# Split products as three matmuls of 256 columns, and new addresses for the weight tiles, in a two-block transformer kernel

## The reference

```
def conv_ffn(h, w_up, conv_w, conv_b, w_down):
    up = causal_dwconv(h @ w_up, conv_w, conv_b)
    a, b = up[..., :FFN_DIM], up[..., FFN_DIM:]
    return (jax.nn.silu(a) * b) @ w_down
```

## Time and profile before

| | |
|---|---|
| time, median of 3 | 2948.65 us (2948.19 to 2951.15) |
| profiled execution, its own time | 2955.68 us |
| its span, first to last instruction | 2953.9 us |
| TensorE busy | 2915.8 us, 99% of the span, 18584 matmuls |
| weight loads busy | 2611.7 us, 88% |
| VectorE / ScalarE / GpSimd busy | 2049.5 / 1311.1 / 69.9 us (69% / 44% / 2%) |
| mean granted TensorE clock | 0.998 of full speed |
| DMA | 531 MB, mean 180 GB/s, about half of the 16 engines' time |

### The profile page before, as it was taken

One profiled execution on the slowest core, in us unless ns is written; L12 is line 12 of the kernel. 1 busy time (PEld: TensorE's weight loads), 2 busy tenths in 40 slices (PEclk: granted clock), 3 DMA queues, 4 the chain that ended last, 5 costly groups with the idle time before them and its releaser, 6 DMA issues.

```text
span 2953.9 us, 47041 instructions
## 1 busy us (share of the span) xinstructions
PE 2915.8 (99%) x18584; PEld 2611.7 (88%) x18584; DVE 2049.5 (69%) x2623; ACT 1311.1 (44%) x1418; POOL 69.9 (2%) x72
## 2 busy tenths in 40 slices
PE   8999999999999999999999999999999999999999
PEld 8898899999988888888888888877988888888888
DVE  6675798877788888885557777637666666665444
ACT  5354423444454444444444345426445444444333
POOL 0000000000001000000000000000000000000000
PEclk9999999999999999999999999999999999999999
DMA  6553334555555555555555555541555555555555
GB/s 233 185 185 134 116 115 157 167 177 190 195 188 196 192 192 196 189 180 186 187 189 202 192 185 177 181 148 72 186 197 187 196 192 191 196 189 180 192 195 185
DMA packets 87998, 531.06 MB, mean 180 GB/s; under 512 B 10080, under 2 KB 10976, under 8 KB 41824
## 3 DMA queue, kind: packets, MB, share of 16 engines
q1 hardware_dynamic: 87904, 529.76, 51.3%
HBM read 527.10 MB, written 2.10 MB: 179 GB/s over the span
## 4 chain that ended last, share of the span: by engine, by line
PE 96%; DVE 3%; ACT 1%; DMA 0%; issue 0%; SPq 0%; DVEq 0%; ACTq 0%
PE bank L594 74%; PE late L594 21%; DVE arena L1703 0%; DVE arena L1700 0%; DVE w_low L1703 0%; DVE half_low L1703 0%; ACT w_high L1219 0%; DVE arena L2005 0%; PE late L1160 0%; DMA ring<-in_w_gates 0%; DMA xT<-in_xT 0%; DVE small L2565 0%; ACT arena L1674 0%; DVE acts_both L1703 0%; DVE arena L2061 0%
## 5 line engine op out<-in xcount | busy, mean ns | idle before, releaser
L1703 DVE TENSOR_TENSOR w_low<-ring,w_high 128x2048 fp32r<-128x2048 f32 (+1 forms) x480 | 1014.2, 2113 | 386.4 <-ACT w_high L1219 382.5
L1219 ACT ACTIVATE w_high<-ring 128x2048 fp32r<-128x2048 f32 (+1 forms) x480 | 849.5, 1771 | 632.9 <-DMA ring<-in_w_down 225.9
L594 PE MATMUL bank<-up_early,w_high 128*128 128x512 f32 x1408 | 487.7, 389 | 0.0
L594 PE MATMUL bank<-up_late,w_high 128*128 128x512 f32 x1408 | 487.3, 389 | 0.0
L594 PE MATMUL late<-acts_both,w_high 128*128 128x512 f32 x1408 | 485.8, 392 | 0.3 <-DVE w_low L1703 0.3
L594 PE MATMUL late<-acts_both,w_low 128*128 128x256 f32 x1408 | 391.7, 278 | 0.0
L594 PE MATMUL bank<-up_late,w_low 128*128 128x256 f32 x1408 | 388.6, 276 | 0.0
L594 PE MATMUL bank<-up_early,w_low 128*128 128x256 f32 x1408 | 388.6, 276 | 0.0
L594 PEld LDWEIGHTS late<-acts_both,w_high 128*128 128x128 f32 x1408 | 264.5, 188 | 58.3 <-DVE w_low L1703 0.6
L594 PEld LDWEIGHTS bank<-up_early,w_high 128*128 128x128 f32 x1408 | 264.3, 188 | 55.1
L594 PEld LDWEIGHTS bank<-up_late,w_high 128*128 128x128 f32 x1408 | 264.3, 188 | 54.8
(11 more groups left out here) (312 smaller groups left out, 4885.0 us busy)
## 6 DMA issues: line engine op xcount, KB each, us to landing
ring<-in_w_up SPq DMA_DIRECT2D x176, 1024.0 KB, 4.7
ring<-in_w_down SPq DMA_DIRECT2D x128, 704.0 KB, 4.0
ring<-in_w_in SPq DMA_DIRECT2D x66, 1024.0 KB, 4.7
ring<-in_w_mix SPq DMA_DIRECT2D x62, 1024.0 KB, 4.8
ring<-in_w_gates SPq DMA_DIRECT2D x96, 512.0 KB, 3.7
ring<-in_w_branch SPq DMA_DIRECT2D x16, 1024.0 KB, 4.8
ring<-in_w_out SPq DMA_DIRECT2D x16, 1024.0 KB, 4.7
ring<-in_w_o SPq DMA_DIRECT2D x16, 1024.0 KB, 4.8
```

The costliest lines, as they stand in the source:

```text
L594: return nc.tensor.matmul(o, lhsT, rhs, start=first, stop=last)
L1219: A(w_high[:, s, 0:cols], ring[:, s, 0:cols], ACT.Copy).then_inc(rounded[s], 1)
L1703: return V.tensor_tensor(o, a, b, op)
```

## The change

Every pair product becomes a triple through `mm3`, including the body of `down`. The bank's second half is no longer written by these products; the copies of it on ScalarE, the adds of the two halves on VectorE and their semaphores (`half_copied`, `gate2_summed`) go, and readers wait for `drained` instead. A pad of 192 bytes behind the ring and a new `arena_pad` move everything behind the ring by 192 bytes: `hT` is at 65856, `arena` at 94784, `w_high` at 192000. Modulo 256 the activations are now at 64, the ring at 128 and `w_high` at 0: lowered weights are 64 off the moving tiles, rounded weights still 192 off, and both halves of the gate units 64 off.

```
+LINE = 16
...
         ring = sb("ring", [P, RING, UNIT])
         ring_base = nc.sbuf_base - RING * UNIT * 4
+        sb("ring_pad", [P, 3 * LINE])
...
-        sb("arena_pad", [P, -nc.sbuf_base % 128 // 4])
+        sb("arena_pad", [P, (hT_base - nc.sbuf_base) % 256 // 4])
...
-            def project_pairs(pairs, waits=None):
-
-                def body(s):
-                    for k in range(KT):
-                        if waits:
-                            waits(k)
-                        c = slice(k * P, (k + 1) * P)
-                        mm(bank[s][:], w_high[:, s, c], pairs[k], k == 0, False)
-                        last = mm(bank[s][:, 0], w_low[:, s, c], pairs[k][:, 0], False, k == KT - 1)
-                    return last
-                return body
...
-                unit_split(project_pairs(pairs, waits))
+                unit_split(project_split(high, low, waits))
...
-                                c = slice(k * P, (k + 1) * P)
-                                mm(bank[4 + b][:], w_high[:, s, c], acts_both[:, :, n], n == 0, False)
-                                last = mm(bank[4 + b][:, 1], w_low[:, s, c], acts_high[:, n], False, n == FF_TILES - 1)
+                                last = mm3(bank[4 + b][:, 0], s, k, acts_high[:, n], acts_low[:, n],
+                                           n == 0, n == FF_TILES - 1)
...
-                unit_split(project_pairs(ups))
-            rounds_split(21, project_pairs(ups))
+                unit_split(project_split(ups_high, ups_low))
+            rounds_split(21, project_split(ups_high, ups_low))
...
-                A(xms[:], bank[s][:, 1], ACT.Copy).then_inc(half_copied, 1)
...
-                link(tt(x, x, bank[4 + b][:, 0:1], ADD))
-                tt(x, x, bank[4 + b][:, 1:2], ADD).then_inc(down_drained[b], 1)
+                tt(x, x, bank[4 + b][:, 0:1], ADD).then_inc(down_drained[b], 1)
...
-                tt(x, bank[s][:, 0], xms[:], ADD).then_inc(drained[s], 1)
+                tt(x, bank[s][:, 0], xrs[:]).then_inc(drained[s], 1)
                 dve.wait_ge(drained[s], units.drained[s].value())
-                link(tt(x, x, xrs[:]))
...
-                tt(o, bank[s][:, 0], in2_rs)
-                tt(xtmp[:], bank[s][:, 1], in2_rs).then_inc(drained[s], 1)
+                tt(o, bank[s][:, 0], in2_rs).then_inc(drained[s], 1)
                 dve.wait_ge(drained[s], units.drained[s].value())
-                return tt(o, o, xtmp[:], ADD)
```

More of the change, by code:

```diff
@@ L270, in build @@
         up_early, up_late = alias("up_early", hT_base, [P, 8, 2, T]), alias("up_late", arena_base, [P, 8, 2, T], 78)
-        ups = [part[:, k] for part in (up_early, up_late) for k in range(8)]
+        ups_high, ups_low = ([part[:, k, n] for part in (up_early, up_late) for k in range(8)] for n in range(2))
         acts_both = alias("acts_both", arena_base, [P, 2, FF_TILES, T], 0)
@@ L661, in _, with merged_out @@
             merges = [0]
-            def merged_out(both):
+            def merged_out(high, low):
                 n = merges[0]
@@ L669, in waits @@
                     pe.wait_ge(merged_lowered, KT * n + k + 1)
-                pairs = [both[:, :, k] for k in range(KT)]
-                unit_split(project_pairs(pairs, waits))
+                unit_split(project_split(high, low, waits))
                 for j in range(3):
-                    unit_split(project_pairs(pairs))
-                rounds_split(3, project_pairs(pairs))
+                    unit_split(project_split(high, low))
+                rounds_split(3, project_split(high, low))
             def project(s):
@@ L1022, in _ @@
             rounds_split(3, branches)
-            merged_out(out_both)
-            raw_unit(lambda waits: project_pairs(ups, waits))
+            merged_out(each(out_high), each(out_low))
+            raw_unit(lambda waits: project_split(ups_high, ups_low, waits))
             for j in range(3):
-                unit_split(project_pairs(ups))
-            rounds_split(21, project_pairs(ups))
+                unit_split(project_split(ups_high, ups_low))
+            rounds_split(21, project_split(ups_high, ups_low))
             down(0)
-            raw_unit(lambda waits: project_pairs(in2, waits), second=True)
-            unit_split(project_pairs(in2))
-            rounds_split(2, project_pairs(in2))
+            raw_unit(lambda waits: project_split(in2_high, in2_low, waits), second=True)
+            unit_split(project_split(in2_high, in2_low))
+            rounds_split(2, project_split(in2_high, in2_low))
             banks_back()
@@ L1500, in round_act, with pair_round @@
                 A(acts_high[:, bass.ds(n, 1)], ACTS[:, bass.ds(n, 1)], ACT.Copy).then_inc(acts_rounded, 1)
[L1502 to L1507, removed]
-                A(xms[:], bank[s][:, 1], ACT.Copy).then_inc(half_copied, 1)
-            def pair_round(i, cols, late, first=False):
+            def pair_round(i, cols, late, convolved, first=False):
                 for j in range(2):
@@ L1515, in pair_round @@
                         root()
-                        act.wait_ge(norm_done, norm[0])
-                    copy_half()
+                    s, _, _, _, _ = units.next()
+                    made = units.drained[s].value()
                     if late[j]:
@@ L1521, in pair_round, with pair_rounds @@
                     round_weights(cols[2 * j + 1])
-                    convs.add()
-                    act.wait_ge(conv_made, convs.value())
+                    if convolved:
+                        convs.add()
+                        act.wait_ge(conv_made, convs.value())
+                    else:
+                        act.wait_ge(drained[s], made)
                     A(cv[:, 2 * j], cv[:, 2 * j], ACT.Silu).then_inc(silu_pair, 1)
-                    copy_half()
+                    units.next()
                     acts.add()
-            def pair_rounds(first, n, late):
+            def pair_rounds(first, n, late, convolved):
                 with act.Fori(0, n) as i:
@@ L1532, in pair_rounds @@
                     acts.enter(i, 2)
-                    convs.enter(i, 2)
-                    pair_round(i + first, [UNIT] * RING, late)
+                    convs.enter(i, 2 * convolved)
+                    pair_round(i + first, [UNIT] * RING, late, convolved)
                 units.leave(n)
@@ L1538, in pair_rounds, with feed_forward @@
                 convs.leave(n)
-            def feed_forward():
+            def feed_forward(convolved):
                 half = SPLIT_UP // 2
[L1542 to L1545, removed]
+                pair_round(0, [UNIT] * RING, (False, True), convolved, first=True)
+                pair_rounds(1, half - 1, (True, True), convolved)
+                pair_round(half, [UNIT] * RING, (True, False), convolved)
+                pair_rounds(half + 1, 20 - half, (False, False), convolved)
                 last = FF_TILES - 2
-                pair_round(21, [UNIT] * 2 + [DOWN * P] * 2, (False, False))
+                pair_round(21, [UNIT] * 2 + [DOWN * P] * 2, (False, False), convolved)
                 act.wait_ge(consumed[(units.pos - 1) % RING], units.consumed[(units.pos - 1) % RING].value())
@@ L1564, in square_of @@
                 norm[0] += 1
+            made2 = []
             for u in range(IN2 + GATES2):
-                units.next()
+                s, _, _, _, free = units.next()
+                made2.append((drained[s], free + 1))
                 if u:
@@ L2210, in low @@
                 def low(n):
-                    lower_raw(n, ups[n][:, 0], ups[n][:, 1], v(gain, n))
+                    lower_raw(n, ups_high[n], ups_low[n], v(gain, n))
                 for n in range(KT):
@@ L2281, in down @@
                     ahead.enter(i, turns=2, drained=0, split=1)
-                    chain.enter(i, 2)
                     turn(i, [DOWN * P] * 8)
@@ L2285, in down @@
                 ahead.leave(7)
-                chain.leave(7)
                 turn(7, [DOWN * P] * 6 + [after] * AHEAD)
@@ L2319, in convolved @@
                 last = stt(o[:, 2:], x[:, 0:T - 2], w(0), o[:, 2:], M, ADD)
-                made_half(last, half)
-            def made_half(last, half):
                 if half == 0:
@@ L2365, in feed_forward @@
                 pairs.leave(20)
-                halves.leave(20)
                 convs.leave(20)
@@ L2600, in _ @@
             residual_raw("g_ffn")
[L2601 removed]
+            feed_forward(scaled, 0, 0)
             down(0)
```

62 lines of the change are left out of this document (24 added, 38 removed).

## The result

The changed kernel takes 3018.36 us (median of 4, 3016.69 to 3026.57) against 2948.42 us before: a ratio of 1.0241, 95% interval 1.0221 to 1.0261. It is slower by 70 us, outside the predicted range (2828 to 2996) and on the side to which I had given 28%.

What follows compares the result with a forecast made beforehand. TensorE was taken as the bound, by matmuls times pace. Terms 0 - 14.1 - 10.2 - 6.8 - 2.7 - 0.4 = -34.2 took the profiled 2955.68 to 2921.5 us (2921 against the median); range 2828 to 2996.

Steps and rivals of the forecast that it cites:

- What bounds the kernel: Whole kernel: TensorE, busy 99% of the span, sets the time by number of matmuls times their start-to-start pace.
- The clean pace of 113.3 ns: Split streams: 256 columns cost 113.3 ns without a clash, so three matmuls take 340 ns.
- faster than a clean pair: Rival, 20%: the new addresses beat a pair's pace, a triple takes 328 ns, total 2834 us.
- Pairs to triples at 340: Pair products, 5664 k tiles: as triples they stay at 340 ns, price 0, bounds 0 to +75.5 us.
- The triples that exist: Existing triples, 1056 k tiles: from 353.3 to 340 ns each, -14.1 us.
- The gates: Gates' half units, 768 k tiles: 360 to 340 ns, 15.4 us of TensorE time, two thirds counted, -10.2 us.
- The slow stretches: First down product and second block's gates: k tiles at 350 return to 340 ns, -6.8 and -2.7 us.
- The last add: Very end of the kernel: the last tile's two adds, 0.88 us, become one, -0.4 us.
- The addresses do nothing: Rival, 11%: paces follow matmul order alone, new triples run at 353.3 ns, old triples and gates unchanged, 3021 us.
- only a linear gain: Rival, 17%: each load's better offset saves only 3.3 ns, a triple takes 350 ns, slower at 2994 us.
- The fixed cost of 2.5 ns a matmul: Rival, 7%, using 2.7 ns: a third matmul adds that, a triple takes 342.7 ns, total 2941 us.

Runs made afterwards that it cites:

- experiment 5: The changed kernel with its two offsets exchanged (rounded weights 64 off, lowered and gates 192 off): 2926.73 us, ratio 0.9916 to the kernel before.
- 13: The kernel of experiment 5 with the gates' rounded half units 64 off as well: 2921.67 us, ratio 0.9899 to the kernel before.
- experiment 10: The changed kernel with a plain float32 matmul of 128 columns ahead of each of the up products' 168 looped units: 2988.58 us, ratio 1.0116 to the kernel before.

## Why the prediction was wrong

- **What bounds the kernel: right.** TensorE is busy for 99% of the span in each of the fifteen profiles and idle for 35 to 40 us of it (38.1 before, 37.2 with the change), at a granted clock of 0.996 to 0.999, the 2.4 GHz level: no wait accounts for the differences, and pace by number of k tiles does.
- **The clean pace of 113.3 ns: right.** 340 is the lowest pace of any form at any offsets, and the triples of experiments 5 and 13 run at it from end to end. The rival "faster than a clean pair" (20%) is refuted as far as these offsets reach.
- **Pairs to triples at 340: wrong, and this is the step that failed**, named as the weak point: "in a stream with locked paces removing the one clash can clear all three". I had seen in the earlier trace rows that a stream has several steady paces, and still gave each form and offset one price. At the changed offsets there are two, 340 and 356.7, and the stream is in the slower one almost everywhere: 1122 k tiles in 400 us of the up product. The term was not 0 but 5664 x 16.7 = +94.6 us less the stretches, more than the 75.5 that I had as its upper bound: that bound came from triples with a load 0 off, on the belief that 64 off could only be better. Against it stands now that 192 / 64 is slower than 192 / 0.
- **The triples that exist: wrong sign**, +3.4 ns a k tile instead of -13.3.
- **The gates: right in size.** 119.3 went to 113.3 in the half unit shown (114.9 on the mean over the stage, since they have two paces as well), and the stage ended 8.3 us sooner, of 11.8 us by the pace (2304 x 5.1 ns): seven tenths, where I had taken two thirds of 15.4.
- **The slow stretches:** they went, but into 356.7. The guess that the timed runs hold the first of them less often than the profiled execution is supported by the later runs of the same kernel, which fall into two groups, 2946 to 2951 and 2953 to 2958 us, 7 apart, as 676 k tiles by 10 ns are.
- **The last add: right**, 0.42 us instead of 0.88.
- **The rivals.** "The addresses do nothing" came nearest in time and is wrong as a cause: with the same instructions, addresses alone move the triple kernel from 2927 to 3061 us. The Trainium skill, SBUF — State Buffer, SBUF: two separate sides, says that TensorE never waits on anyone there. The prediction took from it that addresses could not matter, and that is refuted; whether anything waits at SBUF, and for what, no run here shows. The linear reading of "only a linear gain" had the sign, and fails on experiment 5: by it the clean triple at 64 / 192 leaves nothing for either load to cost at 192 / 64. The fixed cost of 2.5 ns a matmul has no part in it: a triple at 340 has three matmuls in the time of a pair's two. The prediction left out what the same section of the Trainium skill (TensorE: Matmul & The Clock Gate, Back-to-back issue gap) says of that formula: it is the gap of an isolated matmul, and in a stream with weight loads both instructions set the spacing. And the 48 plain products of the earlier trace rows are 24, since the trace shows each as two; the 216 ns are those of one of the two.
- **The chances** gave 72% to cases with a triple at 343 ns or less. Rows showed a stream in two paces at equal addresses; with two paces at hand the chance that the slow one is taken should have been near a half.

Shown: form and offsets act together, several steady paces exist at the same code and offsets within one execution, an interruption can move the stream between them, and at 64 / 192 triples return to 340 by themselves. Not shown: what in the chip clashes. Weight loads and moving reads in each other's way is still my reading; no run separates it from others, and I have no rule that gives the table above from the offsets. Nor is the offset shown to be the right measure: the ring lies at 128 modulo 256 in every run, so the lowered weights' offset and the place of the activations moved together, and all moves are multiples of 64 bytes below 256, so the period of 256 is assumed.

## What to carry to other kernels

In a stream of fp32r matmuls with a weight load each, take the pace from start to start, stage by stage, before costing anything by a count of matmuls, and look for more than one pace at the same code; if there are two, forecast both. Addresses of stationary and moving tiles modulo 256 are worth a scan of a few points on the chip, for the very form of the stream that will run: the best place for one form was the worst for the other, and exchanging two offsets was worth 3%. Judge a place also by whether the stream comes back to the good pace after an interruption, and by the spread of single runs, not by a trace in which it happens to be in it.

## What the runs showed of the hardware

- Split matmuls of 256 columns never ran closer than 113.3 ns on the mean of a unit, 6.2% over the 106.7 ns of their columns at 2.4 GHz, in any of fifteen kernels, while each of the two records of a plain float32 matmul takes 216 ns for 256 columns and 109 for 128 (the extra matmul of experiment 10), which is 2 to 3 ns over two clocks a column.
- Steady paces lie at 340, 346.7, 350, 353.3, 356.7 and 360 ns a k tile, mostly in steps of 3.33 ns, 8 cycles of 2.4 GHz; only 354.7 is off that ladder. The 356.7 is the mean of k tiles of 354 and 359 in turn, and 340 comes as 340 each time.
- At 64 / 192 a stream of triples was back at 340 within five k tiles behind an extra matmul or a wait. Elsewhere a stream kept its pace for as long as nothing else ran on TensorE, its form stayed the same and nothing made it wait, over some 2000 k tiles (0.7 ms). A kernel with 168 additional matmuls was 30 us faster.
